# Mixture-of-experts decoder trunk, one core: joined runs of expert matmuls and an early half chunk of weights

## The reference, cut to what matters

```python
out = jnp.zeros_like(xt)
for e in range(N_EXPERTS):                       # 16 experts
    he = jax.nn.silu(xt @ w_gate[e]) * (xt @ w_up[e])      # 1024 -> 512
    out = out + (he @ w_down[e]) * gate[:, e:e + 1]        # 512 -> 1024
```

## Time and profile before

| What | us |
|---|---|
| median of three runs | 739.78 |
| lowest and highest run | 739.68, 740.61 |
| the profiled execution, its own time | 741.22 |
| the profiled execution, its span from first to last instruction | 739.4 |

### The profile page before, as it was taken

The page is one execution under the profiler, slowest core; times in us unless marked ns, Lnnn a source line. Parts: engine busy times, 40 slices in busy tenths (PEclk is TensorE's granted clock), DMA queues, the critical chain, the costliest instruction groups (busy, mean ns, idle before and its releaser), DMA issues.

```text
span 739.4 us, 9052 instructions
## 1 busy us (share of the span) xinstructions
PE 721.2 (98%) x3696; PEld 391.8 (53%) x3696; DVE 281.5 (38%) x528; ACT 204.0 (28%) x467; POOL 110.1 (15%) x91
## 2 busy tenths in 40 slices
PE   9999999999999999999999999999999999999994
PEld 5877766774344344343368886646434434434331
DVE  4485675363212121121257785526322212112114
ACT  4443689332101110110033555714111011011001
POOL 0011378322000000000052221401200000000001
PEclk9999999999999999999999999999999999999998
DMA  9999900167999999999999964017799999999992
GB/s 329 304 368 418 405 3 1 58 233 297 423 425 429 430 425 429 426 425 422 413 388 387 414 267 187 6 57 285 271 425 428 425 428 428 428 425 429 419 412 84
DMA packets 45596, 245.06 MB, mean 331 GB/s; under 512 B 6256, under 2 KB 10480, under 8 KB 31728
## 3 DMA queue, kind: packets, MB, share of 16 engines
q1 hardware_dynamic: 45552, 244.43, 82.0%
HBM read 243.37 MB, written 1.05 MB: 331 GB/s over the span
## 4 chain that ended last, share of the span: by engine, by line
PE 88%; DVE 6%; ACT 2%; POOL 1%; issue 1%; DMA 1%; SPq 0%; DVEq 0%; ACTq 0%
PE ps L963 30%; PE ps L986 15%; PE ps L883 5%; PE ps L996 4%; PE ps L630 4%; PE ps L632 3%; PE ps L631 3%; PE ps L948 3%; PE ps L776 2%; PE ps L762 2%; PE ps L801 2%; ACT R L1273 1%; PE ps L974 1%; PE ps L939 1%; DVE R L1591 1%
## 5 line engine op out<-in xcount | busy, mean ns | idle before, releaser
L963 PE MATMUL ps<-ring,R 128*64 128x512 f32 x928 | 226.7, 595 | 0.0
L963 PEld LDWEIGHTS ps<-ring,R 128*64 128x64 f32 x928 | 70.3, 137 | 108.8 <-issue 107.2
L986 PE MATMUL ps<-ring,R 128*64 128x512 f32 x448 | 113.4, 595 | 0.8 <-issue 0.8
L1224 ACT ACTIVATE wh<-ps,small 128x512 fp32r<-128x512 f32 x32 | 22.0, 687 | 262.3 <-PE ps L986 260.5
L986 PEld LDWEIGHTS ps<-ring,R 128*64 128x64 f32 x448 | 35.8, 137 | 67.1 <-issue 64.8
L1578 DVE TENSOR_TENSOR wl_r<-ring,wh 128x512 fp32r<-128x512 f32 x72 | 55.4, 787 | 39.7 <-ACT wh L1202 39.3
L1804 DVE SCALAR_TENSOR_TENSOR wl_r<-ps,small,wh 128x512 fp32r<-128x512 f32 x32 | 24.0, 751 | 105.5 <-ACT wh L1224 104.7
L630 PE MATMUL ps<-wh,xh_r 128*128 128x512 f32 x144 | 57.7, 400 | 1.1 <-DVE wl_r L1578 1.0
L1202 ACT CAST wh<-ring 128x512 fp32r<-128x512 f32 x72 | 44.5, 623 | 47.3 <-PE ps L632 45.3
L632 PE MATMUL ps<-wh,xl 128*128 128x512 f32 x144 | 56.3, 391 | 0.0
L631 PE MATMUL ps<-wl_r,xh_r 128*128 128x512 f32 x144 | 56.1, 390 | 0.0
(11 more groups left out here) (237 smaller groups left out, 998.4 us busy)
## 6 DMA issues: line engine op xcount, KB each, us to landing
ring<-in_w_gate SPq DMA_DIRECT2D x24, 2048.0 KB, 17.5
ring<-in_w_up SPq DMA_DIRECT2D x18, 2048.0 KB, 18.7
ring<-in_w_down SPq DMA_DIRECT2D x18, 2048.0 KB, 19.2
ring<-in_w_in SPq DMA_DIRECT2D x20, 1024.0 KB, 14.4
ring<-in_w_gate SPq DMA_DIRECT2D x16, 1024.0 KB, 15.5
ring<-in_w_down SPq DMA_DIRECT2D x24, 512.0 KB, 20.1
ring<-in_w_up SPq DMA_DIRECT2D x12, 1024.0 KB, 11.5
ring<-in_w_out SPq DMA_DIRECT2D x8, 1024.0 KB, 14.9
```

The costliest lines, as they stand in the source:

```text
L963: last = mm(ps[64 * e:64 * e + 64, to, :], xe[:, j, at + 64 * e:at + 64 * e + 64], slots[e][:, j * UNIT:(j + 1) * UNIT], start=(j == 0), s ...
L986: last = mm(ps[64 * e:64 * e + 64, 2 + w, :], hT[:, k, 64 * e:64 * e + 64], slots[e][:, at:at + UNIT], start=(k == 0), stop=(k == FJ - 1))
```

## The change

In pairs 0 to 5 of each layer TensorE's order becomes: gate, up, combine, `transpose_hidden`, `transpose_gates`, first gather (bank 1), second gather (now into bank 0, after `ht_sb`), down, and then the next pair's gate. Pairs 6 and 7 keep their order. ACT copies the second gather right after silu, ahead of the two `scale_y`, and DVE makes the slot tables after `copy_hidden` instead of before `hidden`. Gate and up matmuls of odd pairs (and gate of even ones) wait for the copies out of their banks.

Chunk 11, pair 1's second down matrix, is split: its first half is loaded into the norm vectors' room as soon as the norm has read them, and `load_half_freed` leaves that half out. The matmul helpers take a function for a chunk's column block instead of a slice of the ring.

```diff
+        ROOM = SLOT + 3
+        room = R5[:, 0:2 * D]
+
+        def chunks_at(what, j):
+            if what[0] == "moe" and what[1] % (6 * PAIRS) == ROOM and j < KJ // 2:
+                return room[:, j * UNIT:(j + 1) * UNIT]
+            return in_slot(what)[:, j * UNIT:(j + 1) * UNIT]
...
+            def load_room(n):
+                l = n // (6 * PAIRS)
+                sp.wait_ge(N.x_ready, ready(2 * l, T - 1, 1))
+                i, k = divmod(n % (6 * PAIRS), 6)
+                sp.dma_start(room, expert_src(l, 2 * i + k % 2, k // 2)[:, 0:2 * D]).then_inc(landing(("moe", n), 0)[0], 16)
...
+                        if h == 0 and what[1] % (6 * PAIRS) == ROOM:
+                            continue
...
                 for n in range(ahead, SLOT + 1):
                     load_expert(6 * PAIRS * l + n)
+                load_room(6 * PAIRS * l + ROOM)
                 load_quarters(6 * PAIRS * l + SLOT + 1)
...
+                    def gates_of_pair():
+                        pe.wait_ge(rd.gp, g + 1)
+                        if i:
+                            pe.wait_ge(rd.y_lo, 2 * n)
+                        transpose_gates(rd, 2 * (i % 2))
+
                     for w, done in ((0, rd.gate_done), (1, rd.up_done)):
                         for e in range(2):
                             pe.wait_ge(*landing(chunks[2 * w + e], 0))
-                        if w and i % 2 and more:
-                            pe.wait_ge(rd.xa, 2 * g + 3)
+                        if i % 2 and more:
+                            pe.wait_ge((rd.xa, rd.xe)[w], 2 * g + 3)
+                        elif i and i % 2 == 0 and w == 0:
+                            pe.wait_ge(rd.xa, 2 * g + 2)
...
-                        if w == 0:
-                            pe.wait_ge(rd.gp, g + 1)
-                            if i:
-                                pe.wait_ge(rd.y_lo, 2 * n)
-                            transpose_gates(rd, 2 * (i % 2))
+                        if w == 0 and not more:
+                            gates_of_pair()
...
                     transpose_hidden(rd)
+                    if more:
+                        gates_of_pair()
...
                     pe.wait_ge(rd.ht_sb, n + 1)
+                    if more:
+                        gather(rd, 0, (2 * part + 2, 2 * part + 3), 4 * SLOTS)
                     pe.wait_ge(rd.gsum, n + 1)
...
-                    if more:
-                        pe.wait_ge(rd.xe, 2 * g + 2 + i % 2 + 1)
-                        gather(rd, 1, (2 * part + 2, 2 * part + 3), 4 * SLOTS)
...
                     silu(rd)
+                    if i // 2 + 1 < DUOS:
+                        part = 2 * (i % 2) + 1
+                        act.wait_ge(rd.gathered, 4 * g + 4 + part + 1)
+                        copy_rows(rd, XeT[(i // 2 + 1) % 2], 0, range(2 * part, 2 * part + 2), 4 * SLOTS)
...
-                    dve.wait_ge(rd.gt, n + 1)
-                    slot_tables(rd, i % 2)
+                    if not more:
+                        dve.wait_ge(rd.gt, n + 1)
+                        slot_tables(rd, i % 2)
...
                     copy_hidden(rd)
+                    if more:
+                        dve.wait_ge(rd.gt, n + 1)
+                        slot_tables(rd, i % 2)
```

More of the change, by code:

```diff
@@ L1 @@
 from collections import namedtuple
+from functools import partial
 from contextlib import ExitStack
@@ L314, in in_slot @@
             return ring[:, n] if n < SLOT else extra
+        ROOM = SLOT + 3
[4 more added lines that the diff above has]
+            return in_slot(what)[:, j * UNIT:(j + 1) * UNIT]
+        spare_slots = [lambda j, n=n: ring[:, n, j * UNIT:(j + 1) * UNIT] for n in range(6)]
         def landing(what, h):
@@ L963, in to_hidden @@
                         last = mm(ps[64 * e:64 * e + 64, to, :], xe[:, j, at + 64 * e:at + 64 * e + 64],
-                                  slots[e][:, j * UNIT:(j + 1) * UNIT], start=(j == 0), stop=(j == KJ - 1))
+                                  slots[e](j), start=(j == 0), stop=(j == KJ - 1))
                 last.then_inc(done, 1)
@@ L984, in from_hidden @@
                     for e in range(2):
-                        at = (2 * k + w) * UNIT
-                        last = mm(ps[64 * e:64 * e + 64, 2 + w, :], hT[:, k, 64 * e:64 * e + 64], slots[e][:, at:at + UNIT],
+                        last = mm(ps[64 * e:64 * e + 64, 2 + w, :], hT[:, k, 64 * e:64 * e + 64], slots[e](2 * k + w),
                                   start=(k == 0), stop=(k == FJ - 1))
@@ L1008, in experts @@
                     chunks = [("moe", 6 * n + k) for k in range(6)]
-                    slots = [in_slot(c) for c in chunks]
+                    slots = [partial(chunks_at, c) for c in chunks]
                     more = i // 2 + 1 < DUOS
                     part = 2 * (i % 2)
+                    def gates_of_pair():
[3 more added lines that the diff above has]
+                        transpose_gates(rd, 2 * (i % 2))
                     for w, done in ((0, rd.gate_done), (1, rd.up_done)):
@@ L1065, in spare_round @@
                     pe.wait_ge(rd.w, 96 * n1)
-                    to_hidden(0, XeT[0], 0, [ring[:, 0], ring[:, 1]], rd.gate_done)
-                    to_hidden(1, XeT[0], 0, [ring[:, 2], ring[:, 3]], rd.up_done)
+                    to_hidden(0, XeT[0], 0, spare_slots[0:2], rd.gate_done)
+                    to_hidden(1, XeT[0], 0, spare_slots[2:4], rd.up_done)
                     pe.wait_ge(rd.gp, n1)
@@ L1073, in spare_round @@
                     pe.wait_ge(rd.ht_sb, n1)
-                    from_hidden(rd, [ring[:, 4], ring[:, 5]])
+                    from_hidden(rd, spare_slots[4:6])
                     combine(rd, 0, (pe.snap(2 * i + 2 * PAIRS * rho + 1), pe.snap(2 * i + 2 * PAIRS * rho + 2)))
@@ L1242, in experts @@
                     scale_y(rd, 1)
[L1243 to L1246, removed]
                 return most
```

## The result

The changed kernel took 736.16 us, the median of 10 runs (734.51 to 738.76), beside 740.36 us for the kernel before (10 runs, 739.68 to 742.69). The ratio is 0.9945, with a 95% interval of 0.9929 to 0.9961: 4.1 us faster, where 7.3 had been forecast. The forecast time, 732.5 us, and its range up to 735.4 both missed. The profiled run took 738.76 us for its span of 737.0. Executions of one kernel differ by up to 4.3 us here, which is why the interval is wide.

The account below looks back on a forecast made before the run. TensorE was taken to set the time, with the weight stream only 1.6 us behind per layer. Saving 0.61 us in each of 12 pairs gave 7.3 us off the 739.78 us median: 732.5 us, range 731.2 to 735.4.

Parts of the forecast that it names:

- TensorE's order: Pairs 0 to 5 of each layer: six junctions become two, saving 0.61 us per pair, 7.3 us over 12 pairs.
- the two joins: Gate to up, and down to the next gate, run without a break: 0.15 us each, 0.30 us per pair.
- The estimate from the Trainium skill: Four removed junctions per pair at 0.166 us each: 0.66 us per pair, 8.0 us in all.
- New waits: Second gather waits for DVE's copy, down for the slot tables: covered by 0.3 and 0.6 us.
- C: The new wait for DVE's copy or the tables shows: 0.3 us per pair, 3.6 us back, 736.1 us; 9%.
- D: Slower: the down matmuls wait for the slot tables outright, about 742 us; 2%.
- The half chunk in the room: 1 MB loaded in the DMA gap at 171 to 175 us makes every later chunk 2.45 us earlier.
- The lower bound: 0 instead of 2.45 us: a later transfer, issued only when TensorE frees its place, comes too late and the gap reopens.
- Slack: At pair 7's last up half: 1.6 us to spare per layer, 4.0 with the room; TensorE there 3.7 us early.
- rival B: The stream binds: the earlier MB is given back, each layer keeps 1.6 us, 3.2 in total, 736.6 us; 11%.
- half-kept case: Within B, half of the MB's gain is kept: 2 x (1.6 + 1.2) = 5.6 us, so 734.2 us.

Follow-up runs that it names:

- the last version: Changed kernel with chunk 20's first half sent early into the half place chunk 11 no longer uses; 734.09 us, median of 6 runs, ratio 0.9916.

## Why the prediction was wrong, step by step

**TensorE's order: right.** Forecast 0.61 us per pair; measured 0.63 in pairs 1 to 5, and 7.65 us in all where 7.3 were forecast. Down to the next gate took 6.92 us as forecast. Every term came out: gate, up and down together went from 3 x 7.02 = 21.06 to 13.83 + 6.92 = 20.75 us, so the two joins gave 0.31 (0.30 forecast). Both kinds of transposes went from 0.72 to 0.57, so 0.15 (0.13), and the two gathers from 1.13 + 1.14 = 2.27 to 2.09, so 0.18 (0.18). The estimate from the Trainium skill, "TensorE: Matmul & The Clock Gate", section "Single matmul latency", had been 8.0 us in all. The 7.65 of the runs lie between it and the sum.

**New waits: right.** The covers held. DVE's copy began 0.64 us after the transposes (0.63 forecast), and the tables followed it:

```profile
241.25 0.69 DVE L1822 COPY R<-ps 128x512 f32<-128x512 f32 x1 [1.32 <-PE ps L994]
241.85 0.41 DVE L1826 TENSOR_SCALAR wl_r<-ps 128x256 fp32r<-128x256 f32 x1
242.19 0.41 DVE L1827 TENSOR_REDUCE small<-ps 128x1 f32<-128x256 f32 x1
```

The copy ended at 241.94 and the second gather, the ninth gather step, began at 242.22, so 0.3 us of cover as forecast. The tables ended at 242.60, 0.67 us before down began (0.6 forecast). Rivals C and D fell.

**The half chunk in the room: the failed step.** The words were "so now the issues are well ahead, and I take 2.45". The lower bound had been written down with its mechanism, "the gap reopens there", and that mechanism is what happened: the stream kept 1.2 of the 2.45 us. The prediction set its 2.45 against that by the DMA share over a whole stage, and this share could not tell it. A hole of 1.4 us is 0.7% of 200 us, the share in the earlier trace rows is rounded to 0.01 of 204, 2.0 us, and in full flow it reads 1.01, so 0.98 and 0.99 are not 1 to 2% of idle time either.

What had to be read was the lead of each issue over the landing before it. In the kernel before, chunk 13's first half was issued at 20.9 us and its predecessor landed at 24.5 on the fastest engine, 3.5 us later. With the stream 2.45 us earlier that lead is 1.1, and with down 0.7 us later in pair 0 it is 0.4 (0.55 measured). An issue here needs 1.9 us more than its transfer's 2.48 until it lands (issue at 21.6, landing at 26.0), so 1.35 us of the 2.45 were lost. The Trainium skill, "DMA: Bandwidth & Descriptors", section "Anatomy of one DMA", gives about 2.0 us of fixed cost for a transfer that GpSimd issues. SP issues the ones here, and the trace's 1.9 is near that figure. No such price had been set against the leads. With 3.5 us of lead, 1.9 to start and 0.7 of later down, only 0.9 us of an earlier stream was safe by this estimate. At chunk 13, 0.95 was kept on the fastest engine and 1.2 in the mean.

**Slack and the sum.** The slack of 1.6 us per layer was right: the joins alone brought 1.5. Forecast slack 4.0 against 3.7 needed; measured 1.6 + 1.2 = 2.8 against 3.8. What is missing, 1.0 to 1.3 us per layer, is the wait in pair 7. That is rival B's half-kept case, "2 x (1.6 + 1.2) = 5.6", with a chance of 11% for all of B; the stages show 2.43 + 2.67 = 5.1. Its chance was too small, since the row that decides it was not read.

**From 5.1 to 4.1 us.** The stages lost 5.1 us in the profiled runs and the medians differ by 4.2. 5.1 lies inside the interval of 2.9 to 5.3 us. The profiled run itself gained only 2.5, because its first stage began 2.6 us later, where the clock dipped (told below). On the mean over all runs the clock does not tell the kernels apart (granted 0.9930 and 0.9934 after, 0.9935 before), and the fastest run of each is 5.0 us from the other's (739.50 and 734.51). A stage that waits for the slowest engine scatters with it and one that does not wait keeps its 203.8, which would lower the gain of the median below that of the best runs; this was not shown. So the 3.7 us by which the forecast of 732.5 was short are 7.3 - 5.1 = 2.2 of waiting in the stages, 0.6 because the kernel before took 740.36 in ten runs where the forecast started from 739.78, and 0.9 left open.

## What to carry to other kernels

Where transfers run nose to tail and are issued when a place comes free, an earlier stream is worth only what the thinnest issue allows: list the lead of each issue over the landing ahead of it, subtract what an issue takes to start (1.9 us here), and the smallest rest is about the most that an earlier stream can give (0.9 by that sum here, 0.95 kept on the fastest engine and 1.2 in the mean). A share of 0.99 over a long stage hides such a hole; windows of 5 us show it, and their GB/s more fully than their busy share. And space that an early transfer leaves empty is itself a place for the next one: using it closed the hole without any step being moved.

## What the runs showed of the hardware beside that

**Engines drift apart.** A wait ends with the slowest of 16 DMA engines, and in the changed kernel these were 0.6 to 0.8 us apart right behind the hole and 1.8 to 2.3 at the end of the stage. In other kernels of the study it was up to 4.0 at the end. In the trace, packets of 16 KB of the queue of instructions stand among the weights, about every 25 us, eight to a stage, each holding one engine for 1.0 to 1.1 us, and the landings of single engines step back at these times. From the page, the same in every kernel of this study:

```profile
q8 instruction: 32, 0.52, 0.3%
```

They are 0.3% of the engines' time, but each holds up a single engine. That they cause the drift was not shown: no run moved them. When the stream pauses the slow engines catch up (2.0 us apart ahead of the hole in layer 0, 0.8 behind it), and so a hole hides a part of its price. In the changed kernel the mean landing was 1.2 us earlier than before, the last one 1.0 and 1.1.

**The clock dips in stretches of full work.** TensorE's granted clock fell to its lower level, 1.2 GHz, for 3.4 or 6.8 us at a few places ahead of the stages, in some runs and not in others, in code that the change does not touch. The changed kernel's profiled run, the kernel before, and the last version, the same window of layer 0's mixer:

```profile
88.00:95.00 7.00, 7.00 (x31) 4.52 (x30) 3.65 (x8) 3.51 (x14) 2.60 (x2) 0.56 0.50 211
```

```profile
88.00:95.00 7.00, 6.80 (x51) 4.42 (x50) 4.67 (x9) 5.85 (x25) 3.79 (x2) 1.00 0.52 218
```

```profile
88.00:95.00 7.00, 6.80 (x50) 4.43 (x50) 4.79 (x9) 5.85 (x25) 3.79 (x2) 1.00 0.37 157
```

31 matmuls in the window instead of 50, with TensorE busy in it and before it (7.80 of the 7.80 us up to 88.80), and the stage began at 174.60 us instead of 171.97. What made the clock fall there was not found. Between the stages the dip of the earlier trace rows came in both profiled runs, before and after, 146.3 us each, and not in ten of the eleven others, 145.2. A profiled run is therefore 1 to 3 us off by where its dips fall, which is not small beside the 4.1 us studied here; the stages, in which the clock never fell, compare cleanly to 0.1 us.
